# Two transformer blocks on one core: the three projections that end a block computed with tokens on the partitions

## The reference

```
# block 1                                    # block 2, mixer, then feed-forward
h = rmsnorm(x, pre_g)*(1+scale) + shift      h = rms_norm(x, mix_pre)*(1+sc1) + sh1
...                                          y = merged @ w_out
o = merged @ w_out                           x = x + g1*rms_norm(y, mix_post)
x = x + gate*rmsnorm(o, post_g)              h = rms_norm(x, ffn_pre)*(1+sc2) + sh2
                                             y = (silu(gate)*val) @ w_down
                                             x = x + g2*rms_norm(y, ffn_post)
```

## Time and profile before

| | us |
|---|---|
| median of three runs | 2432.67 (2429.74 to 2435.85) |
| the profiled execution's own time | 2428.56 |
| its span | 2426.8 |
| PE busy | 2282.6 (94%) |
| DVE busy | 1739.9 (72%) |
| ACT busy | 1125.8 (46%) |
| out1, 624.70 to 727.10 | 102.40 |
| out2, 1527.80 to 1631.60 | 103.80 |
| down, 2155.30 to 2413.40 | 258.10 |
| boundary after out1, with kv2 | 47.90 |
| boundary after out2, with the first group of up | 47.80 |
| from the last matmul of down to the end of the span | 13.4 |

### The profile page before, as it was taken

The page is one execution under the profiler, slowest core; times in us unless marked ns, Lnnn a source line. Parts: engine busy times, 40 slices in busy tenths (PEclk is TensorE's granted clock), DMA queues, the critical chain, the costliest instruction groups (busy, mean ns, idle before and its releaser), DMA issues.

```text
span 2426.8 us, 31281 instructions
## 1 busy us (share of the span) xinstructions
PE 2282.6 (94%) x12880; PEld 1970.8 (81%) x12880; DVE 1739.9 (72%) x2018; ACT 1125.8 (46%) x1432; POOL 74.0 (3%) x96
## 2 busy tenths in 40 slices
PE   5499999999997999999999899898999999999998
PEld 3488888888786878888888788787888888888887
DVE  6958877778876777757777888767877777764443
ACT  3243356654454554434555534454444444444442
POOL 0000000001000000000011100000000000000000
PEclk8599999999998999999999999999999999999999
DMA  9887878878883756669767778984555555565553
GB/s 382 318 302 267 309 243 292 285 270 293 292 289 133 251 169 223 233 216 314 262 234 234 260 280 303 326 279 140 191 188 181 187 191 186 181 224 174 186 178 105
DMA packets 245123, 580.57 MB, mean 239 GB/s; under 512 B 11754, under 2 KB 14622, under 8 KB 240756
## 3 DMA queue, kind: packets, MB, share of 16 engines
q1 hardware_dynamic: 232608, 535.93, 64.0%
q0 software_dynamic: 11184, 40.20, 4.9%
q10 hardware_dynamic: 1188, 2.44, 0.3%
HBM read 557.55 MB, written 20.97 MB: 238 GB/s over the span
## 4 chain that ended last, share of the span: by engine, by line
PE 76%; DVE 12%; DMA 8%; ACT 2%; issue 2%; DVEq 0%; SPq 0%; ACTq 0%
PE gemm L1724 44%; PE gemm L1725 22%; DVE w_lo L1072 4%; DMA mod_stage<-in_w_mod 3%; PE gemm L1728 3%; DMA w_stage<-in_w_ada 3%; DVE mod_acc L1066 2%; DMA mod_stage<-in_w_ada 2%; PE gemm L1727 1%; PE extra L1524 1%; PE extra L1517 1%; ACT w_hi L704 1%; DVE mod_acc_scale L1050 1%; PE extra L1656 1%; PE extra L1632 1%
## 5 line engine op out<-in xcount | busy, mean ns | idle before, releaser
L1724 PE MATMUL gemm<-operand_main,w_hi 128*128 128x512 f32 x4311 | 1558.7, 403 | 44.6 <-DVE proj L1398 20.8
L1725 PE MATMUL gemm<-operand_main,w_lo 128*128 128x256 f32 x4311 | 1216.8, 282 | 0.0
L1072 DVE TENSOR_TENSOR w_lo<-w_stage,w_hi 128x1024 fp32r<-128x1024 f32 x736 | 860.8, 1211 | 445.0 <-ACT w_hi L704 444.5
L704 ACT ACTIVATE w_hi<-w_stage 128x1024 fp32r<-128x1024 f32 x736 | 732.4, 1044 | 746.8 <-PE gemm L1725 714.2
L1724 PEld LDWEIGHTS gemm<-operand_main,w_hi 128*128 128x128 f32 x4311 | 820.1, 190 | 236.5 <-DVE w_lo L1072 33.1
L1725 PEld LDWEIGHTS gemm<-operand_main,w_lo 128*128 128x128 f32 x4311 | 823.6, 191 | 13.3
L1066 DVE SCALAR_TENSOR_TENSOR mod_acc<-mod_stage,c_silu,mod_acc 128x1024 f32<-128x1024 f32 x210 | 267.2, 1299 | 56.6 <-DMA mod_stage<-in_w_mod 40.8
L1724 PE MATMUL gemm<-ffn_hidden,w_hi 128*128 128x512 f32 x688 | 242.9, 397 | 0.0
L1725 PE MATMUL gemm<-ffn_hidden,w_lo 128*128 128x256 f32 x688 | 192.5, 280 | 0.0
L1724 PE MATMUL gemm<-operand_attn,w_hi 128*128 128x512 f32 x480 | 176.5, 408 | 16.0 <-DVE proj L1398 10.1
L1724 PEld LDWEIGHTS gemm<-ffn_hidden,w_hi 128*128 128x128 f32 x688 | 129.1, 188 | 29.4
(11 more groups left out here) (213 smaller groups left out, 1453.5 us busy)
## 6 DMA issues: line engine op xcount, KB each, us to landing
w_stage<-in_w_in SPq DMA_DIRECT2D x128, 1024.0 KB, 7.1
mod_stage<-in_w_mod SPq DMA_DIRECT2D x192, 512.0 KB, 5.9
w_stage<-in_w_up SPq DMA_DIRECT2D x88, 1024.0 KB, 5.0
w_stage<-in_w_down SPq DMA_DIRECT2D x44, 1024.0 KB, 5.0
w_stage<-in_w_merge SPq DMA_DIRECT2D x32, 1024.0 KB, 5.6
w_stage<-in_w_out SPq DMA_DIRECT2D x32, 1024.0 KB, 7.5
w_stage<-in_w_ada SPq DMA_DIRECT2D x31, 1024.0 KB, 7.8
mod_stage<-in_w_ada SPq DMA_DIRECT2D x32, 512.0 KB, 5.8
```

Of the source, the lines that this page charges most:

```text
L704: return nc.scalar.activation(o, i_, f, **kw)
L1072: tt(WL[:, slot_of(n), c0:c1], WST[:, slot_of(n), c0:c1], WH[:, n % HIS, c0:c1].bitcast(F32), ALU.subtract)\
L1724: mm(G[:, m, :], hi, x_of(k), start=(k == 0), stop=False)
L1725: ins = mm(G[:, m, T:2 * T], lo, x_of(k)[:, 0:T], start=False, stop=False)
```

## The change

The 76 slabs of `out1`, `out2` and `down` swap the roles of the operands. The tokens are the stationary operand (128 of them at a time) and the weights move, 512 columns at a time; x_hi is loaded twice, x_lo once. Output, residual and o lie in rows (tokens on the partitions), so that a sum over channels is a sum along the row of one engine's instruction. A group needs two banks, and the groups take the pairs (0, 1) and (2, 3) in turn.

```diff
+            def gemm_rows(n, ph, g, q, nk, x_of):
+                last = q == g.slabs - 1
+                order = [(kc, h) for h in range(2) for kc in range(QUAD)] if last else [(kc, h) for kc in range(QUAD) for h in range(2)]
+                for kc, h in order:
+                    k = q * QUAD + kc
+                    if k == 0:
+                        wait_banks(g, h)
+                    o = row_bank(g, h)
+                    hi, lo = WH[:, n % HIS, 512 * kc:512 * kc + 512], WL[:, slot_of(n), 512 * kc:512 * kc + 512]
+                    x_hi, x_lo = x_of(k)[:, h * P:(h + 1) * P], x_of(k)[:, T + h * P:T + (h + 1) * P]
+                    mm(o, x_hi, hi, start=(k == 0), stop=False)
+                    mm(o, x_hi, lo, start=False, stop=False)
+                    ins = mm(o, x_lo, hi, start=False, stop=(k == nk - 1))
```

At a group's end ACT squares the bank and sums along the row (o.o); DVE multiplies the bank by the gain row (gate times norm weight) into p; for the two boundaries ACT squares p with a sum (p.p) and DVE multiplies x by p with a sum (x.p). With r = 1/rms(o) the square sum of the new x is x.x + 2r x.p + r^2 p.p, so the second norm doesn't wait for the new x:

```diff
+            def gain_rows(g):
+                    dve.wait_ge(gain_in, 16 * (k + 1))
+                    dve.wait_ge(start["resid_in"], 16 * (k + 1))
...
+                    tt(p, row_bank(g, h), GAIN[rows_of(k)][:, columns_of(r)], ALU.mult).then_inc(pair_done, 1)
...
+                        stt(JUNKD[:, h, :], ROWX[0][:, h, columns_of(r)], 1.0, p, ALU.mult, ALU.mult, accum_out=S_XP[:, h, r:r + 1])\
...
+                    link(tt(T1, V_PP, R1V, ALU.mult))
+                    link(stt(T1, V_XP, 2.0, T1, ALU.mult, ALU.add))
+                    link(tt(T1, T1, R1V, ALU.mult))
+                    link(tt(SXX, SXX, T1, ALU.add))
...
+                    root_of(n + 1, SXX, R2V)
+                    norm_rows(k, 0)
```

```diff
-            def sums(n, c, sq, tiles, first, last):
-            def token_sums(c, sq, tiles, first, last):
-            def turn(src, src0, tiles, at0):
+            def turn_rows(k, c):
+                pe.wait_ge(y_made, 8 * k + 2 * c + 2)
...
+                if what == "prep_h" and k:
+                    turn_rows(k - 1, 0)
+                    turn_rows(k - 1, 1)
                 if what == "resid" and k < 2:
...
+                    mod_end(4 * k + 4)
...
+                    if ph.name in ("kv2", "up") and ph.i == 0 and s < 2:
+                        turn_rows(int(ph.name == "up"), s + 2)
```

POOL's queue: the 2 MB store of the transposed x at the start goes (with DVE's wait for it), the gain goes out as 2048 elements of 4 bytes and comes back as a row broadcast to all partitions (1 MB), ahead of the residual:

```diff
-            pool.dma_start(resid.rearrange("t q n -> q t n"), PROJ[:, XT0:XT0 + KT, :]).then_inc(start["x_t_stored"], 16)
+            def store_gain(k):
+                pool.wait_ge(out_aff, k + 1)
+                pool.dma_start(gains[k].rearrange("(t q) -> q t", q=P), AFF[:, 2 * KT:3 * KT], allow_slow_non_contiguous=True)\
+            def load_gain(k):
+                pool.wait_ge(gains_stored, 16 * (k + 1))
...
+                pool.dma_start(GAIN[rows_of(k)][:, :], gains[k].partition_broadcast(P)).then_inc(gain_in, 16)
...
+                if ph.name in ("branch1", "branch2") and i == 3:
+                    store_gain(int(ph.name[-1]) - 1)
+                if ph.name == "up" and i == 1:
+                    store_gain(2)
```

More of the change, by code:

```diff
@@ L719, in _ @@
             activate(AFF[:, 0:2 * KT], COL[:, 0:2 * KT], ACT.Sigmoid).then_inc(c_ready, 1)
+            act.wait_ge(const_set, 2)
+            act.wait_ge(start["x_in"], 16)
+            for h in range(2):
+                positive(act, x_sq, h)
+                activate(MST[:, :, :].rearrange("q a n -> q (a n)"), XTOK[:, h, :], ACT.Square, accum_out=SXX[:, h:h + 1]).then_inc(x_sq, 1)
             for b in range(8):
```

451 lines of the change are left out of this document (224 added, 227 removed).

## The result

The changed kernel takes 2399.45 us (median of four runs, 2392.9 to 2403.88), the kernel before 2434.26 beside it (2429.74 to 2442.29): the ratio is 0.9851, with a 95% interval of 0.9812 to 0.9890. So it is faster by 35 us, where I had forecast 59 (2374 from 2432.67), and it lies above my range, which ended at 2392. The profiled execution took 2403.51, 25 us less than that of before: its 2428.56 was faster than each of the four timed beside the change, and this one is among the slowest of its own.

What follows compares the result with a forecast made beforehand. PE, busy 94%, was taken to bound the kernel as a stream of matmuls. Out1 10.8, out2 10.7, down 11.8, boundaries 21.8 and tail 1.9 made 57.0 us: 2375.7 on the median's scale, forecast 2374, range 2353 to 2392.

Steps and rivals of the forecast that it cites:

- the charge for what is late next: In out1 and out2, DVE's longer queue delays `w_lo` and the gain adds loads: 2 us charged each (0 to 9).
- point 3: Out1 and out2: waits for a bank at group starts vanish, giving 7.3 and 7.2 us, less 2 each for later lateness.
- point 4: Boundaries after out1 and out2: PE restarts after 10.6 us instead of 23.8; 37.0 for 47.9, gaining 10.9 each.
- rival B: Out1 and out2 bound by loads and DVE, 98 to 100 us each, whole 2382 to 2390; chance 0.15 (2386 to 2400).
- Rival C: Gain's store of 4-byte elements (13.7 to 219 us) makes the gain late for out1 and out2, kernel slower; chance 0.03.
- Point 1: Slabs of out1, out2 and down: PE pays by the column, 5.60 us a slab for 5.63, 1.3 us in down.
- Rival A: PE faster than by the column, 0.2155 us a matmul, 5.17 a slab, 33 us less: 2343; chance 0.14 (below 2360).
- Point 2: PE's hooks of sums and transposes go from out1, out2 and down: 5.0, 5.0 and 10.5 us gained.
- only h=1 counts: Boundary chain: half h=0 of the last group finishes half a slab earlier, so only the other half delays PE.
- Point 5: Tail after down: the eight additions start 2.3 us after the last matmul instead of 4.25, gaining 1.9 (1.5 to 2.5).
- Point 6: Store of x, two ACT squares, the gain's tiny product and ACT's table load: no cost; an exposed table load 1.3 each.
- The sum: Whole kernel: gains of 10.8, 10.7, 11.8, 21.8 and 1.9 make 57.0 us, 2375.7 on the median's scale; forecast 2374.

Runs made afterwards that it cites:

- e_nostore: Changed kernel without the store of the gain, the norm's weight broadcast in its place (gate missing from the result): 2382.37 us.
- e_rowstore: Changed kernel with the gain transposed on PE and stored as 16 rows of 512 bytes, not 2048 4-byte elements: 2386.93 us, 0.9792 of the kernel before.
- a_again: The changed kernel once more, nothing edited, as yardstick: 2397.91 us, ratio 0.9852 to the kernel before.
- e_split256: Changed kernel with every 512-column matmul in down made two of 256, same columns and result: 2414.96 us.
- e_both: Changed kernel with the gain stored in rows and a third of out1's and out2's modulation rows moved ahead: 2365.38 us, 0.9708 of the kernel before.
- e_onebank: e_both with the alternation of banks undone in out1 and out2, every group using banks 0 and 1: 2381.26 us.
- e_moverows: Changed kernel with a third of out1's and out2's modulation rows moved ahead into branch1, gates2 and branch2: 2387.24 us.
- e_shortrows: Changed kernel with DVE using 128 of each 1024 columns of modulation rows in out1 and out2, all loads kept (result incomplete): 2378 us.
- e_halfbytes: Changed kernel with modulation row loads in out1 and out2 carrying 64 of 128 partitions, half the bytes (result incomplete): 2382 us.

## Why the prediction was wrong, point by point

**The step that failed is the charge for what is late next, in point 3:** "I charge 2 us to each phase for that (0 to 9)", with its companion in point 4, that the chain of a boundary starts 0.85 after the last matmul. What I had as rival B, at 0.15, is the case, and it is worse than I priced it because it doesn't end with the stage. Beyond the 2 us charged, out1 fell short of its forecast by 6.4 and out2 by 11.1, the store's part (below) included; then DVE took up the last bank 8.4 after the last matmul where I had 0.85, and kv2's first matmul came 18.2 after it for 10.6; both are some 7.5 late, which I had not carried over: 5.6 and 7.4 of the boundaries' gain were lost. B's signs were the right ones, waits for `w_out` slabs and `w_lo`, and its 98 to 100 us for a phase is near out1 (97.9, then 99.5) and short of out2's first profile (104.2, then 101.4); its DMA share of 0.95 wasn't reached (0.87 and 0.85). That the whole, 2399, lies in B's 2386 to 2400 is in part luck: 9.7 of the shortfall stands in stages that B doesn't touch, and down and the tail made 8.2 of it good. My reason for B's size was wrong too: I divided bytes by 341 GB/s, while a window here moved 385, and the limit is a ring of two buffers and three in-order queues, in which DVE's own passes count beside the loads. The profile of before gave reason to ask: its groups of 24.3 held slabs, a hook and the rows; I took 2.5 us of PE's work out of them without asking what else took nearly 24.3.

**Rival C had about the right price, by luck, and the wrong victim.** I reckoned 13.7 us for the store and found it hidden, since nobody waits for the gain. The store took 13.4 and the gain indeed wasn't late. But the reckoning took each element for a packet of 107 ns, and the trace has 144 packets more with the three stores than without (e_nostore), 48 a store, not 2048: the price was right for a wrong reason. And the store held up the other loads, which cost 5.5 us in out1's first group and 5.1 to 6.7 in out2's (e_nostore and e_rowstore against a_again). The Trainium skill's page "DMA: Bandwidth & Descriptors", section Specifications, wants 512 bytes or more for the line rate. The trace agrees for the store itself; what it adds is the price for the others, 45 to 89 GB/s for all queues together while the store lasts.

**Point 1, the pace:** right in sign, mis-sized. I chose 5.60 a slab, by the column; it is 5.44, my lower bound of 5.42 within 0.02. That 512 and 256 columns cost in proportion, my reason for going by the column and against a fixed cost, was read from starts that differ by 0.23 and 0.11 or 0.12; measured over whole slabs they are 0.227 and 0.120, which aren't in proportion. Down gave 18.7, not 11.8: less the 10.5 of the hooks, the pace gave 8.2 where the sum has 1.3. The fixed 13.3 ns makes 32 matmuls dearer than 24 by 0.11 a slab, 4.7 in down, and the rest of the difference is that the old stream ran at 5.65 in many slabs, where its own form gives 5.55; I haven't found why. Rival A's pace (0.2155) didn't come, and a load that shows the more the less its matmul covers is ruled out by e_split256. The Trainium skill's page "TensorE: Matmul & The Clock Gate", section Back-to-back issue gap, gives 2.5 ns beyond the columns for an isolated warm matmul. The streams here, with a load for each matmul, have 13.3 in the new form and 13 to 17 in the old (5.55 to 5.65 a slab).

**Point 2, the hooks:** right. With the rows out of the way the groups are at 21.76 and nothing of the hooks is left.

**Point 3, the banks:** right in what the banks bring: 17.2 us in out1 and out2 between e_both and e_onebank, 13.5 with the boundaries, where I had 13.5 for the waits and the cold starts. What fails of point 3 is the charge above.

**Point 4, the boundaries:** the chain is right where DVE is on time. In both boundaries of e_onebank and the second of e_moverows DVE takes up the first half of the group 1.6 to 2.0 before the last matmul's end and the second 0.81 to 0.82 after it (0.85 forecast), and the first slab matmul comes 10.5 to 10.7 after it (10.6 forecast). Those boundaries take 35.1 to 36.0 for a forecast of 37.0, because the group behind takes 24.6 to 25.5, not 26.4: PE came out of the transposes at nearly full clock. In e_both, at 38.2 and 36.8, DVE is still late: it takes up the last bank 4.0 and 2.6 after the last matmul, and the first slab matmul comes at 13.8 and 12.2. That this is near 37.0 is two errors that cancel. When DVE is late both halves stand one after the other (2.9 us from the first to the end of the second in the rows above, with 0.78 of waiting for ACT, whose second square stands behind the square of p), and "only h=1 counts" no longer holds.

**Point 5, the tail:** the additions start 2.1 after the last matmul, forecast 2.3; the rest of the 3.2 gained lies behind them, between the last addition and the last landing.

**Point 6, edits at nothing:** none of the edits that it lists was found to cost anything. Of the 9.7 us of "all else" 7.8 stand behind a `mod_end` and are clock: 3.0 in merge's first group, 1.6 in the first slab of branch1, 3.2 in branch2 (2.7 for that stage as a whole). The store isn't the cause in branch2: the stage takes 151.4 without it, but also 151.0 to 151.2 in three profiles with it (e_split256, e_shortrows, e_halfbytes), and 153.3 with the store in rows. Whether the change brings the low clock on stays open; merge's first group had it in every profile of a changed kernel and in neither of the old one, branch2 in some.

**The sum.** With most of both losses taken out, e_both's 2365 is 9 less than my 2374; that it comes so near is in part the pace of down, which the forecast had too small. What the forecast lacked was two things: a supply chain that had been about as slow as the work above it, and a small transfer that blocks large ones.

## What to carry to other kernels

When a change takes work off the bounding engine, look at each stage for the next chain that fills the same time, and read its length from its own period (buffers, queues passed in order, the passes inside), not from bytes over bandwidth; a stage whose two chains are about equally long hardly shows the second. Such a lateness doesn't stay in its stage: whatever follows in the same queue starts late, and the price of a boundary depends on who arrives at it on time. A transfer that nobody waits for can still cost the others, if it is cut into thousands of elements (11 us here between a_again and e_rowstore); turn it on PE first, and store it in rows.
